# Down projections of a two-layer transformer step: 9 of 22 chunk pairs as seven block products for eight

## The reference

```
def conv_ffn(h, w_gate, w_up, conv_w, conv_b, w_down):
    a = causal_dwconv(h @ w_gate, conv_w, conv_b)
    return (jax.nn.silu(a) * (h @ w_up)) @ w_down
...
h = rmsnorm(x, g[2])
x = x + rmsnorm(conv_ffn(h, ...), g[3])
```

## Time and profile before

| what | value |
|---|---|
| median of 3 runs | 2115.18 us (2114.7 to 2115.31) |
| span of the profiled execution, first to last instruction | 2113.3 us |
| first down stage in the trace | about 748.2 to 993 us |
| second down stage in the trace | about 1856 to 2102 us |
| TensorE, VectorE, ScalarE, GpSimd busy | 100%, 63%, 50%, 14% of the span |

### The profile page before, as it was taken

How to read it: one execution, slowest core, us unless ns; L and a number is a source line. 1 busy time by engine, 2 the same in 40 slices (tenths; PEclk the granted TensorE clock), 3 DMA queues, 4 the chain that set the end, 5 groups by cost and what they waited for, 6 DMA issues and landing times.

```text
span 2113.3 us, 34635 instructions
## 1 busy us (share of the span) xinstructions
PE 2104.6 (100%) x12177; PEld 1803.3 (85%) x12177; DVE 1336.3 (63%) x2048; ACT 1064.2 (50%) x1627; POOL 286.4 (14%) x461
## 2 busy tenths in 40 slices
PE   9999999999999999999999999999999999999999
PEld 9987888888888888888999977888888888888887
DVE  7665676766766754445876654576766767754444
ACT  6675554444444444434666776554444444444443
POOL 4452000000000000000065773000000000000000
PEclk9999999999999999999999999999999999999999
DMA  7444455555565565554773334455565565565554
GB/s 256 151 159 154 166 194 194 181 191 187 172 204 181 187 213 187 188 188 155 235 251 121 101 111 135 155 200 189 179 193 184 180 199 186 182 215 190 188 187 133
DMA packets 111008, 381.42 MB, mean 180 GB/s; under 512 B 14194, under 2 KB 18754, under 8 KB 110402
## 3 DMA queue, kind: packets, MB, share of 16 engines
q1 hardware_dynamic: 108466, 373.63, 53.6%
q10 hardware_dynamic: 2448, 6.53, 0.9%
HBM read 377.97 MB, written 2.14 MB: 180 GB/s over the span
## 4 chain that ended last, share of the span: by engine, by line
PE 97%; DVE 1%; ACT 1%; DMA 0%; issue 0%; ACTq 0%; DVEq 0%
PE set L764 32%; PE set L842 30%; PE set L768 16%; PE set L1058 10%; PE set L1132 2%; PE set L900 1%; PE set L1106 1%; PE set L1154 1%; PE set L932 1%; PE set L1108 1%; PE set L1156 0%; PE set L974 0%; DVE wlo L1851 0%; PE set L1222 0%; PE set L1223 0%; DMA raw<-in_stream 0%
## 5 line engine op out<-in xcount | busy, mean ns | idle before, releaser
L1851 DVE TENSOR_TENSOR wlo<-raw,whi 128x1024 fp32r<-128x1024 f32 x703 | 859.9, 1233 | 560.1 <-ACT whi L1389 558.3
L1389 ACT ACTIVATE whi<-raw 128x1024 fp32r<-128x1024 f32 x703 | 736.9, 1056 | 725.8 <-PE set L768 351.2
L764 PE MATMUL set<-hs,whi 128*128 128x512 f32 x2896 | 952.7, 395 | 0.6 <-ACT whi L1487 0.3
L768 PE MATMUL set<-hs,wlo 128*128 128x256 f32 x2896 | 681.9, 281 | 0.0
L768 PEld LDWEIGHTS set<-hs,wlo 128*128 128x128 f32 x2896 | 534.8, 188 | 60.0 <-DVE wlo L1851 0.2
L764 PEld LDWEIGHTS set<-hs,whi 128*128 128x128 f32 x2896 | 497.2, 189 | 69.8 <-issue 0.8
L842 PE MATMUL set<-whi,hid 128*128 128x512 f32 x1360 | 374.6, 395 | 0.0
L842 PEld LDWEIGHTS set<-whi,hid 128*128 128x128 f32 x1360 | 255.1, 188 | 63.6 <-DVE wlo L1851 0.6
L842 PE MATMUL set<-wlo,hid 128*128 128x512 f32 x680 | 215.8, 395 | 0.0
L1058 PE MATMUL set<-hs,whi 128*128 128x256 f32 x1280 | 213.3, 286 | 0.3 <-DVE wlo L1851 0.3
L1058 PEld LDWEIGHTS set<-hs,whi 128*128 128x128 f32 x1280 | 176.6, 189 | 3.0 <-DVE wlo L1851 1.1
(11 more groups left out here) (219 smaller groups left out, 1449.0 us busy)
## 6 DMA issues: line engine op xcount, KB each, us to landing
raw<-in_stream SPq DMA_DIRECT2D x703, 512.0 KB, 3.4
gain_rows<-rows ACTq DMA_DIRECT2D x4, 1024.0 KB, 5.9
xT<-in_x SPq DMA_DIRECT2D x8, 256.0 KB, 7.7
out_y<-out_f SPq DMA_DIRECT2D x8, 256.0 KB, 2.4
bo_rows<-rows ACTq DMA_DIRECT2D x1, 768.0 KB, 9.1
wg_raw<-in_w_gates ACTq DMA_DIRECT2D x1, 768.0 KB, 4.6
raw<-in_stream SPq DMA_DIRECT2D x2, 256.0 KB, 4.3
bo_last<-rows ACTq DMA_DIRECT2D x1, 256.0 KB, 11.7
```

The lines of the kernel that those rows point to most:

```text
L764: return mm(sets[set_of(u)][:, t, 0:2 * w], whi[:, slot, cols], r, start=first, stop=final)
L768: return mm(sets[set_of(u)][:, t, w:2 * w], wlo[:, slot, cols], r[:, 0:w], start=False, stop=False)
L1389: A(whi[:, slot, :], raw[:, slot, :], ACT.Copy).then_inc(hi_ready, 1)
L1851: V.tensor_tensor(wlo[:, slot, :], raw[:, slot, :], whi[:, slot, :].bitcast(F32), ALU.subtract).then_inc(lo_ready, 1)
```

## The change

The two units of a pair (1024 output columns) are worked on together: `DOWN_ORDER` interleaves the 44 chunks of the pair, and nine times a chunk c of the first unit and the chunk c of the second stand together in slots 0 and 1 (FOLDED), followed by two plain chunks in slots 2 and 3. Such a pair of chunks is a product of a 2x2 grid of blocks (two halves of the tokens by two k-tiles) with a 2x2 grid of blocks (two k-tiles by two groups of 512 columns): eight block products of three matmuls each. The changed kernel forms it from seven block products, with four sums of activation blocks (`fold_h`) and four sums of weight blocks (`fold_w`), which GpSimd makes; they are split into high and low parts on ScalarE and VectorE, and partial products gather in the four banks of `sets[1]`. VectorE joins these into `y` (`sum_shares`), which is then added to the result of the plain banks like a bias (`bias_y`). There are four such pairs of units in the program, 36 folded pairs of chunks in all.

```
+FOLDED = range(4, 21, 2)
+PLAIN = [c for c in range(CHF) if c not in FOLDED]
+DOWN_START, DOWN_END = 4, 5
+DOWN_ORDER = [(0, c) for c in PLAIN[:DOWN_START]]
+for q, c in enumerate(FOLDED):
+    DOWN_ORDER += [(0, c), (1, c), (0, PLAIN[DOWN_START + q])]
+    if q < len(FOLDED) - 1:
+        DOWN_ORDER += [(1, PLAIN[q])]
+DOWN_ORDER += [(1, c) for c in PLAIN[-DOWN_END:]]
...
+            def fetch_down(u):
+                for i, (k, c) in enumerate(DOWN_ORDER):
+                    g = first_chunk(u) + i
+                    before = fold_at(i - RING)
+                    if before is None:
+                        sp.wait_ge(lo_ready, g - RING + 1)
+                    else:
+                        sp.wait_ge(fold_w_made, 4 * (folds_before(u) + before + 1))
+                        sp.wait_ge(lo_ready, first_chunk(u) + FIRST_FOLD + RING * before + CK)
+                    sp.dma_start(raw[:, g % RING, :], stream[first_chunk(u + k) + c]).then_inc(raw_in[g % RING], 16)
...
+            def fold_operands(u, n):
...
+                nc.gpsimd.tensor_tensor(hid_sum[:], hid[:, kt:kt + CK, 0:S].bitcast(F32),
+                                        hid[:, kt:kt + CK, S:2 * S].bitcast(F32), ALU.add).then_inc(fold_h_step, 1)
+                pool.wait_ge(raw_in[0], 16 * turns)
+                pool.wait_ge(raw_in[1], 16 * turns)
+                if q > 0:
+                    pool.wait_ge(fold_used, 5 * (q - 1) + 2)
+                nc.gpsimd.tensor_tensor(fold_w[:, 0], w22, w12, ALU.subtract).then_inc(fold_w_made, 1)
+                if q > 0:
+                    pool.wait_ge(fold_used, 5 * (q - 1) + 4)
+                pool.wait_ge(fold_h_step, 3 * q + 1)
+                nc.gpsimd.tensor_tensor(fold_h[:, 0], h21, h22, ALU.add).then_inc(fold_h_step, 1)
+                nc.gpsimd.tensor_tensor(fold_h[:, 2], h11, h21, ALU.subtract)
+                pool.wait_ge(fold_h_step, 3 * q + 2)
+                nc.gpsimd.tensor_tensor(fold_h[:, 1], fold_h[:, 0], h11, ALU.subtract).then_inc(fold_h_step, 1)
+                pool.wait_ge(fold_h_step, 3 * q + 3)
+                nc.gpsimd.tensor_tensor(fold_h[:, 3], h12, fold_h[:, 1], ALU.subtract).then_inc(fold_h_made, 1)
+                if q > 0:
+                    pool.wait_ge(fold_w_low, 4 * (q - 1) + 2)
+                nc.gpsimd.tensor_tensor(fold_w[:, 1], w12, w11, ALU.subtract).then_inc(fold_w_made, 1)
+                pool.wait_ge(fold_w_made, 4 * q + 2)
...
+                nc.gpsimd.tensor_tensor(fold_w[:, 2], w22, fold_w[:, 1], ALU.subtract).then_inc(fold_w_made, 1)
+                pool.wait_ge(fold_w_made, 4 * q + 3)
...
+                nc.gpsimd.tensor_tensor(fold_w[:, 3], w21, fold_w[:, 2], ALU.subtract).then_inc(fold_w_made, 1)
...
+            def folded_down(u, n, g):
...
+                pe.wait_ge(lo_ready, g + CK)
+                pe.wait_ge(fold_h_low, q + 1)
+                product(sets[0][:, 2, :], fold_h_hi[:, 3], fold_h_lo[:, 3], whi[:, 1, lower], wlo[:, 1, lower],
+                        first, False).then_inc(fold_used, 1)
+                pe.wait_ge(fold_w_low, 4 * q + 1)
+                share(3, 2, fold_w_hi[:, 0], fold_w_lo[:, 0]).then_inc(fold_used, 1)
+                pe.wait_ge(fold_w_low, 4 * q + 2)
+                share(2, 0, whi[:, 1, upper], wlo[:, 1, upper]).then_inc(fold_used, 1)
+                pe.wait_ge(fold_w_low, 4 * q + 3)
+                share(1, 1, fold_w_hi[:, 1], fold_w_lo[:, 2]).then_inc(fold_used, 1)
+                pe.wait_ge(fold_w_low, 4 * q + 4)
+                product(sets[0][:, 1, :], *tile(1, 1), fold_w_hi[:, 2], fold_w_lo[:, 3], False, False).then_inc(fold_used, 1)
+                product(sets[1][:, 0, :], *tile(0, 0), whi[:, 0, upper], wlo[:, 0, upper], first, final)
+                product(sets[0][:, 0, :], *tile(1, 0), whi[:, 0, lower], wlo[:, 0, lower], False, False).then_inc(chunk_used, CK)
...
             def bias_y(u, n, k, t):
 
-                bias_row = (bo_last[:] if k == 3 else bo_rows[:, k * UNIT:(k + 1) * UNIT]).rearrange("p (a f) -> p a f", a=CK)
+                if is_down(u):
+                    dve.wait_ge(shares_summed, 5 * (2 * (u >= DN1) + k // 2 + 1))
+                    bias_row = y[:, CK * k:CK * (k + 1), t, :]
```

More of the change, by code:

```diff
@@ L229, in build_program @@
         with ExitStack() as c:
+            fold_w = sb("fold_w", [4, UNIT], F32, c)
+        with ExitStack() as c:
+            fold_w_lo = sb("fold_w_lo", [4, UNIT], F32R, c)
+        with ExitStack() as c:
             turned = sb("turned", [2, 2, CAUSAL], F32, c)
@@ new lines, in plain_down @@
+            def plain_down(u, k, c, g, first, last):
+                if last:
+                    turns = [(j, t, i) for t in range(TT) for j in range(CK) for i in range(3)]
+                else:
+                    turns = [(j, t, i) for j in range(CK) for i in range(3) for t in range(TT)]
+                if first:
+                    pe.wait_ge(evacuated, UT * (u - 1))
+                pe.wait_ge(lo_ready, g + 1)
+                for j, t, i in turns:
+                    cols = slice(j * UNIT, (j + 1) * UNIT)
+                    part = slice(S * (i == 2) + t * P, S * (i == 2) + (t + 1) * P)
+                    w = wlo if i == 1 else whi
+                    final = last and j == CK - 1 and i == 2
+                    starts = first and j == 0 and i == 0 and (k, t) != (1, 0)
+                    ins = mm(sets[0][:, CK * k + t, :], hid[:, CK * c + j, part], w[:, g % RING, cols], start=starts, stop=final)
+                    if final and t == 0:
+                        ins.then_inc(y_first, 1)
+                ins.then_inc(chunk_used, 1)
@@ new lines, in down_pair @@
+            def down_pair(u, layer, between=None):
+                held = len(DOWN_ORDER) - HELD
+                for i, (k, c) in enumerate(DOWN_ORDER):
+                    g = first_chunk(u) + i
+                    if between and i >= held:
+                        break
+                    if u in (DN0, DN1):
+                        if i == 0:
+                            pe.wait_ge(hid_ready, NF * layer + NF - 2)
+                        elif c // 2 >= NF - 2:
+                            pe.wait_ge(hid_ready, NF * layer + c // 2 + 1)
+                    n = fold_at(i)
+                    if n is None:
+                        last = i + 1 in (DOWN_FIRST_DONE, len(DOWN_ORDER))
+                        plain_down(u + k, k, c, g, (k, c) in ((0, 0), (1, 0)), last)
+                    elif k == 0:
+                        folded_down(u, n, g)
+                if between:
+                    last_chunks(u + 1, 1, hid, [(first_chunk(u) + i, DOWN_ORDER[i][1]) for i in range(held, len(DOWN_ORDER))],
+                                between)
@@ L883, in between_last, with last_chunks @@
                     last_bank(0, 1)
-            def last_chunks(u, k, source, n, between):
+            def last_chunks(u, k, source, held, between):
                 for t in range(TT):
-                    for c in range(n - HELD, n):
-                        g = first_chunk(u) + c
+                    for m, (g, c) in enumerate(held):
+                        last = m == len(held) - 1
                         if t == 0:
@@ new lines, in down_pair @@
+            def down_pair(u, evacs, norm_next=False):
+                g0, n = first_chunk(u), len(DOWN_ORDER)
+                for f in range(FOLDS):
+                    fold_split(u, f)
+                for i in range(FIRST_FOLD + RING * FOLDS, DOWN_FIRST_DONE + RING - 1):
+                    split(g0 + i)
+                sum_shares(u)
+                evacs[0]()
+                for i in range(DOWN_FIRST_DONE + RING - 1, n if u == DN1 + 2 else n + 1 if norm_next else n + RING - 1):
+                    split(g0 + i)
+                evacs[1]()
+                if not norm_next:
+                    split(g0 + n + RING - 1)
@@ L2058, in last_norm @@
                 scale_y(u_last, n, 3, 0)
[L2059 removed]
+                bias_y(u_last, n, 3, 1)
+                dve.wait_ge(y_scaled, 23)
                 for c in range(6, CH):
```

207 lines of the change are left out of this document (167 added, 40 removed).

## The result

The changed kernel takes 2250.53 us (median of 4 runs, 2248.37 to 2253.08), the one before beside it 2114.94 (2114.53 to 2115.31): a ratio of 1.0641, 95% interval 1.0626 to 1.0656. It is 135.6 us slower. 156 were predicted, 2271 us in all, with a range of 2195 to 2325. The span went from 2113.3 to 2249.6 us.

The account below looks back on a forecast made before the run. TensorE's matmul count was taken to bound the kernel before, a load, sums and splits loop the changed one. 180 us of turns and first folds, less 25.2, plus 1.4, made +156 on 2115.2: 2271 us, range 2195 to 2325.

Parts of the forecast that it names:

- TensorE is the bound, and loses 108 matmuls: Down stages: 21 matmuls in place of 24 in each of 36 folded pairs, at 0.233 us, 25.2 us off.
- GpSimd and VectorE exclude each other: Folds: GpSimd's SBUF reads and VectorE's two-input instructions exclude each other, over 14 us a turn against TensorE's 10.5.
- The loop closes through the load: Folds: load, sums, splits, next load form a loop without TensorE; slot 1 lands 5.0 us after slot 0's issue.
- whoever has its next instruction ready keeps the right of way: Between VectorE and GpSimd in a fold: gives turns of 16.0 us, TensorE waiting 5.5 in each; chance 0.62.
- taking turns by order of issue: Rival in the folds: engines alternate by issue order, a turn of 14.4 us, 2224 us in all; chance 0.15.
- a fourth sum of 1.8 us: Sign in the next profile that the engines take turns: length of each fold's last weight sum.
- The first fold of a layer: First fold of each pair of units: adds 1 to 2 us, its own sums taking 13.5 us from the stage's start.
- `sum_shares`: nothing: Tails: five VectorE instructions under plain chunks, 14 us of TensorE, cost nothing.
- The clock: Forecast 1.00; rival: TensorE's stops lower it, half of the turns longer, 2350 us, sign two matmul distances; chance 0.08.

Follow-up runs that it names:

- run 2: Changed kernel with each of GpSimd's nine sums replaced by two `memset`s that only write, so the sums aren't computed: 2151.09 us, ratio 1.0172.
- run 10: Changed kernel with the two products that need no sum first, slots released earlier, and the next activation sum after the weight sums' low parts: 2236.49 us, ratio 1.0575.
- run 4: Kernel before the change, with the 20 copies of 16 coefficients made as two-input sums with a zero tile: 2118.91 us in a single run.
- run 3: Changed kernel, but at each layer's first folded pair GpSimd makes the four weight sums before waiting for all of `hid`: 2250.02 us, ratio 1.0643.
- Run 7: Changed kernel with 4 folds to a pair, one to every eight chunks, and the five `sum_shares` additions spread behind the last splits: 2150.95 us, ratio 1.0162.
- run 9: Kernel with one fold to eight chunks (2151.65 us), GpSimd's next activation sum waiting for the low parts of the fold's weight sums: 2136.67 us, ratio 1.0105.
- Run 11: Changed kernel with 5 folds to a pair, one to six chunks, additions spread, sum-free products first and the next activation sum later: 2127.77 us, ratio 1.0063.
- run 8: Changed kernel with 5 folds to a pair, one to every six chunks, and the five `sum_shares` additions spread: 2165.39 us, ratio 1.0238.

## Why the prediction was right, and where it wasn't

**TensorE is the bound, and loses 108 matmuls: right.** Outside the stops and the stretches of the lower clock the matmuls stand 0.233 us apart, as before.

**GpSimd and VectorE exclude each other: right**, by the rows of the turn and by run 2 against the changed kernel, for 70 to 99 us.

**The loop closes through the load: right.** 4.7 us from issue to the first sum (5.0 predicted for slot 1's landing), 9.5 us of sums and splits; a load that came 2.9 us later lengthened its turn by 2.6; and run 10 left the turn at 14.29.

**Who has the right of way: wrong.** The step that failed is "whoever has its next instruction ready keeps the right of way". It gave a turn of 16.0 us and a last weight sum that waits for four splits. Measured: 14.29 us, the last weight sum 1.60 us long, let in after one split. In 72 cases in the folds GpSimd's instruction was issued inside one VectorE instruction and ahead of a next one that was itself issued before the first had ended; GpSimd went ahead of that next one in all 72. That is the first of the listed rivals, taking turns by order of issue, whose turn was worked out at 14.4 us. Its sign, a fourth sum of 1.8 us, came as 1.6. The Trainium skill, "SBUF — State Buffer", section "Who interferes with whom", says "Issue order, not op shape, decides who blocks"; the folds agree with that sentence. I had set it aside for 20 copies that do lose, in 18 cases of 20, in every kernel here. Why these lose is open: run 4 rules the number of inputs out, the rows of run 3 the idle time ahead of them and the moment of issue, and in the kernel before other GpSimd instructions in attention did get in between two splits. Their size, 16 columns, is untested. 20 cases from one place in the program were taken for the rule of all places.

**Sizes.** A turn costs 3.8 us over TensorE's 10.5 in place of 5.5, and 32 of them, a few longer, 127 us in place of 176. The rival's time, 2224 us, was still 26 too low, since both had these too small:
- *The first fold of a layer*, "adds 1 to 2": it stopped TensorE 8.8 and 8.7 us from start to start, 17 in all. The sums were counted from the stage's start at 748.6; they wait for the last of `hid`, made at 757.7. Run 3 shows that moving them forward isn't enough. The second pairs' first folds added 5.
- *`sum_shares`: nothing.* It is 3.4 us of VectorE in a row, with `bias_y` behind, and TensorE then waited 1.6 us for a split. The tails cost 4.5 us more than before. Run 7 shows that spreading the five alone doesn't give this back. `bias_y` was put at 0.69 us twice. Outside the two stages the span grew by 1.4 us, but unevenly: 1.1 behind the second stage, 0.2 between the two and 0.1 ahead of them, so the match of the sum is chance in part.
- *The clock.* Granted 0.50 in 19 stretches within the two stages, of 3.4 to 10.2 us, first from 763.5, inside TensorE's first long stop; matmuls stand 0.43 us apart there, in place of 0.233. Nearly all lie inside turns in which TensorE waits anyway, and the turn keeps its 14.3 us, the first one too. Some 7 us were lost where it doesn't wait, in the plain chunks behind each pair's last fold (1.5 to 2.2 us, four times). The forecast was a clock of 1.00, and the sign of the rival, two matmul distances, came; the longer turns that it priced did not.

Together 127 + 17 + 5 + 4.5 + 7 = 161 us of TensorE's time, less 25.2, plus the 1.4 outside the stages: 137, measured 136.3. Two errors in opposite directions (49 us too much for the turns, 29 too little for the rest) left 20 us between forecast and result. That the time came this near is luck: the turn that it rests on did not happen.

**The account I put in its place also had a hole.** I took the turn for filled by the two engines' work and expected it hidden when TensorE asked for longer. At eight chunks to a fold TensorE asks 21.7 us and still lost 2.5 a turn. A fold pays two things: exclusion, part of which fell with the place of one instruction (run 9), and the latency of load, sums and splits in a ring of four slots. Run 11 differs from run 8 by the edits of both run 9 and run 10, so its 37.6 us aren't divided between the two; but the stop at the first sum, which the edit of run 9 alone had left, is gone in 18 of its 20 folds.

## What to carry to other kernels

Work for an idle engine is priced by its chain: from the landing of its data to the first instruction of the bound engine that needs it, against what the ring lets that engine do meanwhile. Put what doesn't depend on the new work first, and let the idle engine's next piece wait until the splits that someone waits for are through. And ask of every row that stands for a rule from how many places in the program it comes.

## What the runs showed of the hardware

- A GpSimd sum of two SBUF inputs took 1.295 us at 512 columns, 0.46 at 128; a `memset` 0.53 and 0.20 at these sizes, and neither it nor the split beside it grew longer.
- In the folds the order of issue decided in all 72 cases; in one loop of the kernel a 16-column copy issued ahead of the second of two splits still waited for both in 18 of 20.
- The granted clock fell to 0.50 inside a stop, or at most 1.3 us behind one, of 2.2 to 8.8 us from start to start, for 3.4 to 10.2 us, and went back up while TensorE still stopped twice in each turn. Many stops of 2.2 to 2.6 us left it at 1.00.
- Two loads of 512 KB issued 0.43 us apart: GpSimd, which needs both, began 4.70 us after the first issue, where a load by itself took 3.3 in the median.
